# A fused three-layer kernel: eight gate tiles moved ahead of a barrier or into an attention's last heads, and one norm's steps drawn later

## The chip, the cores and the metric

The kernel runs on one core of one Trainium2 chip. The metric is the time of one execution on the device, in microseconds (us). The engines are PE (TensorE, matmuls), PEld (its weight loads), DVE (VectorE), ACT (ScalarE), POOL (GpSimd) and SP (which issues most DMA). TensorE's clock is either 1.2 or 2.4 GHz; the profile gives the granted clock of a stretch as a share of the full one.

## The reference, cut to what matters

A first block (one hybrid layer on 512 tokens and 16 meta tokens in front, width 1024), then two latent layers that work on 512 tokens and a context of 256:

```python
h = h + 0.5 * swiglu(rmsnorm(h, norm_ffn1), w_ffn1_in, w_ffn1_out)
u = rmsnorm(h, norm_mix)
fq, fk, fv, ff, rq, rk, rv, rg, ga, gb = split(u @ w_in)
y_a = forgetting_attention(rms(fq), rms(fk), fv, log_sigmoid(ff + b))   # "fox": 16 heads of 64
y_b = silu(rg) * head_groupnorm(retention(rotary(rq), rotary(rk), rv))  # 4 heads, values 256 wide
mixed = sigmoid(ga + b_gate[:D]) * (y_a @ w_o_fox) + sigmoid(gb + b_gate[D:]) * (y_b @ w_o_ret)
h = h + mixed @ w_out
h = h + 0.5 * swiglu(rmsnorm(h, norm_ffn2), w_ffn2_in, w_ffn2_out)
# then, for l in 0, 1: modulate (a LayerNorm without gain, times 1 + scale, plus shift), the projection
# w_in_2, three kinds of mixing, w_o_2, LayerNorm, and a swiglu between two more norms
```

## The kernel before, in words

Activations lie transposed: 128 features on the partitions, 8 blocks of them, tokens along the free axis. A product of such an activation by a weight matrix is made tile by tile: a weight tile has 128 output features and all 8 blocks of input (128x1024 numbers). Every fp32 product is three fp32r matmuls, high by high, high by low and low by high (`mm3`, L1134 to L1137), so a tile of 8 blocks over 512 tokens is 24 matmuls of 512 columns, and one over 256 tokens (a "chunk") 24 of 256.

A weight tile goes through three engines before PE may use it. SP loads it into a ring of four buffers (`Wf`), ACT rounds it to its high half (L1744, `Wbaseh`, `Wtoph`, `Wlatenth` by the region it goes to), DVE subtracts that from the whole and leaves the low half (L2366, `Wbasel`, ...). Both emit the split of a tile in the program order of their own queue, one tile ahead of PE's use of it (`get`), so a split stands in line with whatever else ACT and DVE do at that place.

Each engine has a class that writes its queue by the same method names (`retention`, `mix`, `hooks`), and semaphores tie them together. The order around three places matters here.

**Retention.** The rotated queries and keys (`RQ`, `RK`) and the values (`VR`) are ready behind a barrier (`bar("rot")`, which waits for DVE's and ACT's last writes). Then PE makes 16 scores (L1488, L1490), each for one head and one block of 128 queries, and one step later the output of that unit, once DVE has multiplied the scores by the decay table `DT`. The 8 tiles of the gate `silu(rg)` (weights `w_rg`, 512 tokens) depend on none of this and stand in front of every second output.

**Fox attention and mix.** 64 units, one for each head (16) and block of 128 queries (4). A unit goes round a loop: scores on PE (L1586 to L1589), row maximum on DVE (L2870), exp on ACT (L2118), scaling by the sum on DVE (L2886, `Pb`), transposition on PE (L1601, L1602), copies on ACT (L2132, `PT`; L2133, `MT`). The transposition of unit u stands behind the scores of unit u+1 or so, and after the fourth unit of a head comes the product with the values (L1629). Steps of the projections and norms of later heads are hung between the scores and what follows by lists of hooks (`FOX_PLAN`, run by `hooks`); behind unit 51 hardly any of them are left. Behind the last head comes the mix: for each of the two branches 8 times a gate tile (`w_ga` or `w_gb`, 512 tokens, input `X1`) and an output tile (`w_of` with the attention's output `YA`, or `w_or`), then ACT's sigmoid and DVE's product.

**The norm before the second latent sequence.** Here a planner (`woven`) lays the steps of three LayerNorms (`mean`, `mu`, `sq`, `var`; means L1339, totals L1361, on ones in `CF`) between weight tiles: each chain has a tile after which it may start and a delay in us by which its steps fall due. `FILL` says how many dummy matmuls (L1123, output unused) PE makes in front of a named step, so that it stays busy while it waits. The norm `a0` has chunk 0 for the context and chunks 1 and 2 for the latent tokens; behind chunk 2's last step stand 16 tiles of 256 columns with the normed tokens `X2`, of which the later ones need `X2`'s second half.

Of the kernel before, what the change touches and what calls it, by code (L numbers as in the profile page):

```python
# [502 lines left out]
class Ffn:  # L503
# [12 lines left out]
    def ends(self, c, ci=None):  # L516


        if ci == 2 and self.tag[0] == "g":
# [13 lines left out]
FOX_OWN = (0, 14)  # L533
FOX_CH = {"q": LAT, "k": TWO}
FOX_FIRST = [[("refine", "q", 0), ("root", "k", 0)], [("scale", "q", 0), ("refine", "k", 0)],
             [("root", "k", 1), ("scale", "k", 0)], [("refine", "k", 1), ("scale", "k", 1)]]
# [85 lines left out]
def qk_before(l, s, c):  # L622
# [3 lines left out]

FILL = {("fa", "f1", 0, 0): 7, ("yb", 6): 4, ("mean", "a0", 1): 11, ("mu", "a0", 2): 13, ("hm", 0, 0, 0): 2,
# [173 lines left out]
def second_sequence(p):  # L801

    f, n3, a = p.ffns["f2"], p.norms["n3"], p.norms["a0"]
    items = [(("open", "mixed", [(p.mm, ("branch", 1, 7, 0))]), 0, None)]
    items += [(("wo", m, c), 2.8, None) for m, c in lagged(range(8), 2, 4)]
    ends = [last_of(items, "wo", c, None) for c in (0, 1)]
    items[8:8] = [(("ahead", 2), 0, None)]
    items += [(("close", "mixed"), 0, None), (("open", "top", [(p.mm, ("mixout", 7, 1))]), 0, None)]
    items.append((("vectors", 1), 0, None))
    tiles = ffn_items(f, 4, lambda c: c, mod_steps(1))  # L810
    items += tiles[:8] + [(("ahead", AHEAD), 0, None)] + tiles[8:]
    done = last_of(items, "fb", 1, f)
    ends += [last_of(items, "fo", c, f) for c in (0, 1)]
    items += [(("close", "top"), 0, None), (("open", "latent", [(p.mm, ("fo", "f2", 2, 7, 1))]), 0, None)]
    items += projection_items(0, lambda c: 2 + c)
    chains = [(chain([n3], c), ends[c], 1.9) for c in (0, 1)] + [(chain([a], 0), done, 0.0)]
    chains += [(chain([a], c + 1), ends[2 + c], 0.8) for c in (0, 1)]
    return woven(items, chains)
# [75 lines left out]
class FoxUnits:  # L894
    def __init__(self, p):
        self.p, self.id, self.l, self.units, self.joined, self.lag, self.slots = p, "fox", None, [], True, 2, 4
        late = fox_steps(False)
        for h in range(16):
            sel, v = p.SEL[:, h, :].bitcast(BF16), h // 2 * 128
            for i in range(4):  # L900
# [12 lines left out]
                d.head_done = i == 3  # L913
                d.hooks = [("fox", *x[1:]) for x in late if x[0] == 4 * h + i]
                self.units.append(d)
# [170 lines left out]
class TensorE(Engine):  # L1086
# [369 lines left out]
    def retention(self):  # L1456
        p, e = self.p, self.e
        for s in range(4, 12):
# [6 lines left out]
            if s <= 8:  # L1465
                self.ret_turn(s - 1)
        self.bar("rot")
        e.wait_ge(*p.dve.of(("bar", "rot")))
        e.wait_ge(*p.act.of(("bar", "rot")))
        for u in range(17):  # L1470
            if u < 16:
                self.ret_scores(u)
                if u % 2 == 0:
                    self.lin("w_rg", (u // 2,), 8, p.X1, 0, [(16, 512)], ("rg", u // 2),
                             lambda c: (p.act, ("rg", u // 2)))
            if u >= 1:
                self.ret_out(u - 1)
        self.features(p.YT, range(4), range(8), ("yb",), lambda f: (p.dve, ("yb", f)),
                      lambda f: [(p.dve, ("gn", f // 2, 3))])
        self.bar("yb")  # L1480

    def ret_scores(self, u):
# [44 lines left out]
    def fox_step(self, m, f, *a):  # L1527
        if f == "project":
            self.project(a[0], m, *a[1:])
        elif f == "root":  # L1530
            self.root(a[0], m, a[1])
        elif f == "stack" and 2 * m + a[0] not in FOX_OWN:
            self.p.stacks[2 * m + a[0]] = self.used + AHEAD + NW + 1
# [87 lines left out]
    def head_values(self, A, u):  # L1621
# [8 lines left out]
        t.then_inc(*p.mm.did(("c", A.id, h)))  # L1630

    def mix(self):
        p, e = self.p, self.e
        for br, (wg, wo, Y) in enumerate((("w_ga", "w_of", p.YAs), ("w_gb", "w_or", p.YBs))):
            for m in range(8):
                self.lin(wg, (m,), 8, p.X1, 0, LAT, ("gate", br, m), lambda c: (p.act, ("gate", br, m)))
                self.lin(wo, (m,), 8, Y, 16, LAT, ("branch", br, m), lambda c: (p.dve, ("branch", br, m)),
                         (lambda c0, n, k: [(p.dve, ("ysplit", br, k))]) if m == 0 else None)
            if br == 0:
                self.bar("m1")  # L1640
# [89 lines left out]
class ScalarE(Engine):  # L1730
# [313 lines left out]
    def fox_step(self, m, f, *a):  # L2044
        if f == "project":
            self.project(a[0], m, *a[1:])
        elif f == "root":
            self.root(a[0], m, a[1])
        elif f == "stack":
            self.stack(2 * m + a[0])  # L2050

    def project(self, which, m, i, k0, k1):
# [108 lines left out]
    def mix(self):  # L2161
        p, e = self.p, self.e
        for br, (wg, wo, Y, S, G) in enumerate((("w_ga", "w_of", p.YAs, p.YA, p.GT),
# [3 lines left out]
            for m in range(8):  # L2167
                self.lin(wg, (m,))
                self.lin(wo, (m,))
# [185 lines left out]
class VectorE(Engine):  # L2355
# [440 lines left out]
    def fox_step(self, m, f, *a):  # L2796
# [4 lines left out]
        elif f == "scale":  # L2801
            self.head_scale(a[0], m, a[1])
        elif f == "stack" and 2 * m + a[0] in FOX_OWN:
            self.stack(2 * m + a[0])

    def stack(self, h):
# [5 lines left out]
        e.tensor_tensor(p.KL[o:o + 64, s, :], p.K[r0:r0 + 64, m % 2, :], p.KS[r0:r0 + 64, s, :].bitcast(F32),  # L2812
                        ALU.subtract).then_inc(*p.dve.did(("sk_low", h)))

    def project(self, which, m, i, k0, k1):
# [129 lines left out]
    def mix(self):  # L2945
        p, e = self.p, self.e
        for br, (wg, wo, Y, S, G) in enumerate((("w_ga", "w_of", p.YAs, p.YA, p.GT),
# [3 lines left out]
            for m in range(8):  # L2951
                self.lin(wg, (m,))
                self.lin(wo, (m,))
# [663 lines left out]
```

## Time and profile before

| | us |
|---|---|
| median of 3 runs | 3371.64 (3370.69 to 3379.82) |
| the profiled execution, its own time | 3374.06 |
| its span, first to last instruction | 3372.0 |
| DVE busy | 1695.1 (50%) |
| ACT busy | 1333.7 (40%) |
| POOL busy | 475.1 (14%) |
| mean granted clock of TensorE | 0.995 |

The span is what the trace covers; 2.1 us of the execution lie outside it. The times of the trace count from the span's start. PE is busy nearly all of the time, so the stretches in which it has no real work are few: idle gaps, dummy matmuls, and stretches at half clock. A row of the timeline shows in brackets how long its engine was idle before it and which instruction ended that.

### The profile page before, as it was taken

The page shows a single profiled execution, that of the slowest core. Times are in us where ns is not written, and L with a number is a line of the kernel's source. Part 1 is how long each engine was busy: PE and PEld are TensorE (multiplying, and loading weights), DVE is VectorE, ACT ScalarE, POOL GpSimd, SP SyncE. Part 2 cuts the span into 40 slices and gives each one's busy share as a digit, 9 for nine tenths or more (in the row PEclk, how much of TensorE's full clock was granted, in tenths as well). Part 3 has the DMA queues.
Part 4 walks back from the last instruction along what each step waited for, and adds up shares of the span by engine and source line. Part 5 has one row for each costly group of instructions (what it writes and reads, how often), then busy time and mean ns, then how long its engine had stood idle before and what let it go on. Part 6 is the DMA issues. An engine that isn't in the chain of part 4 may idle for free. (4 is left out here: it accounts for less than half of the span.)

```text
span 3372.0 us, 60102 instructions
## 1 busy us (share of the span) xinstructions
PE 3268.7 (97%) x24738; PEld 3046.1 (90%) x24754; DVE 1695.1 (50%) x2839; ACT 1333.7 (40%) x2350; POOL 475.1 (14%) x471
## 2 busy tenths in 40 slices
PE   8999999999899999999999999999999999999998
PEld 7999988887678999998889889999998889999997
DVE  4666643546634456666445773222227646743234
ACT  4222322346633332225347664212125547552224
POOL 1010110036400010010013201001010114110100
PEclk9999999999999999999999999999999999999999
DMA  4444422122122244443201431111214212423222
GB/s 162 159 171 172 138 82 76 54 74 66 36 88 94 100 136 177 169 170 99 67 30 38 128 101 57 63 57 58 69 56 133 85 55 48 152 70 91 91 93 91
DMA packets 94973, 325.23 MB, mean 96 GB/s; under 512 B 10800, under 2 KB 15152, under 8 KB 94576
## 3 DMA queue, kind: packets, MB, share of 16 engines
q1 hardware_dynamic: 90992, 307.19, 28.1%
q0 software_dynamic: 3280, 13.68, 1.2%
q8 instruction: 199, 3.26, 0.4%
q14 instruction: 70, 0.57, 0.1%
q10 hardware_dynamic: 432, 0.52, 0.0%
HBM read 309.96 MB, written 2.10 MB: 93 GB/s over the span
## 5 line engine op out<-in xcount | busy, mean ns | idle before, releaser
L2366 DVE TENSOR_TENSOR r_Wbasel<-r_Wf,r_Wbaseh 128x1024 fp32r<-128x1024 f32 (+1 forms) x298 | 378.0, 1269 | 549.8 <-ACT r_Wbaseh L1744 549.3
L1744 ACT ACTIVATE r_Wbaseh<-r_Wf 128x1024 fp32r<-128x1024 f32 (+1 forms) x298 | 308.4, 1039 | 447.1 <-PE PS L1137 351.4
L1135 PE MATMUL PS<-r_X1h,r_Wbaseh 128*128 128x264 f32 (+2 forms) x1216 | 392.0, 322 | 13.1 <-POOL r_X1l L3192 3.4
L1135 PE MATMUL PS<-r_X2h,r_Wbaseh 128*128 128x256 f32 (+1 forms) x1224 | 373.8, 305 | 5.7 <-POOL r_X2l L3192 3.1
L1136 PE MATMUL PS<-r_X1l,r_Wbaseh 128*128 128x264 f32 (+2 forms) x1216 | 378.6, 311 | 0.0
L1137 PE MATMUL PS<-r_X1h,r_Wbasel 128*128 128x264 f32 (+2 forms) x1216 | 378.0, 311 | 0.0
L1137 PE MATMUL PS<-r_X2h,r_Wbasel 128*128 128x256 f32 (+1 forms) x1224 | 366.7, 300 | 0.0
L1136 PE MATMUL PS<-r_X2l,r_Wbaseh 128*128 128x256 f32 (+1 forms) x1224 | 364.3, 298 | 0.0
L2366 DVE TENSOR_TENSOR r_Wtopl<-r_Wf,r_Wtoph 128x1024 fp32r<-128x1024 f32 (+1 forms) x165 | 200.1, 1214 | 275.9 <-ACT r_Wtoph L1744 275.7
L1135 PEld LDWEIGHTS PS<-r_X1h,r_Wbaseh 128*128 128x128 f32 x1216 | 230.1, 189 | 37.4 <-issue 8.7
L1135 PE MATMUL PS<-r_X2h,r_Wtoph 128*128 128x256 f32 x872 | 248.1, 285 | 2.1 <-POOL r_X2l L3192 2.1
L1135 PEld LDWEIGHTS PS<-r_X2h,r_Wbaseh 128*128 128x128 f32 x1224 | 230.8, 189 | 19.6 <-POOL r_X2l L3192 4.3
L1137 PE MATMUL PS<-r_X2h,r_Wtopl 128*128 128x256 f32 x872 | 247.4, 284 | 0.0
L1136 PE MATMUL PS<-r_X2l,r_Wtoph 128*128 128x256 f32 x872 | 247.4, 284 | 0.0
L1136 PEld LDWEIGHTS PS<-r_X1l,r_Wbaseh 128*128 128x128 f32 x1216 | 230.4, 189 | 14.5 <-issue 2.4
L1137 PEld LDWEIGHTS PS<-r_X1h,r_Wbasel 128*128 128x128 f32 x1216 | 230.7, 190 | 13.0
L1136 PEld LDWEIGHTS PS<-r_X2l,r_Wbaseh 128*128 128x128 f32 x1224 | 232.7, 190 | 10.4 <-issue 2.6
L1137 PEld LDWEIGHTS PS<-r_X2h,r_Wbasel 128*128 128x128 f32 x1224 | 230.0, 188 | 7.9
L1744 ACT ACTIVATE r_Wtoph<-r_Wf 128x1024 fp32r<-128x1024 f32 (+1 forms) x165 | 168.7, 1027 | 169.0 <-PE PS L1137 83.9
L1951 ACT ACTIVATE r_TM<-PS 128x256 f32<-128x256 f32 (+1 forms) x198 | 76.0, 385 | 339.0 <-PE PS L1137 334.0
L1135 PE MATMUL PS<-r_X1h,r_Wtoph 128*128 128x264 f32 (+1 forms) x672 | 190.4, 283 | 4.7 <-DVE r_Wtopl L2366 4.6
L2615 DVE TENSOR_TENSOR r_TM<-r_TM,PS 128x256 f32<-128x256 f32 (+1 forms) x198 | 83.3, 421 | 216.7 <-PE PS L1137 203.7
(428 smaller groups left out, 9078.5 us busy)
## 6 DMA issues: line engine op xcount, KB each, us to landing
r_Wf<-in_wmod SPq DMA_DIRECT2D x96, 512.0 KB, 3.6
r_Wf<-in_f_in SPq DMA_DIRECT2D x88, 512.0 KB, 4.4
r_Wf<-in_g_in SPq DMA_DIRECT2D x88, 512.0 KB, 3.5
r_Wf<-in_g_out SPq DMA_DIRECT2D x56, 448.0 KB, 3.3
r_Wf<-in_w_o SPq DMA_DIRECT2D x40, 512.0 KB, 4.3
r_Wf<-in_f_out SPq DMA_DIRECT2D x32, 448.0 KB, 4.2
r_Wf<-in_f_out SPq DMA_DIRECT2D x16, 512.0 KB, 4.4
r_Wf<-in_w_v SPq DMA_DIRECT2D x16, 512.0 KB, 3.5
```

The source lines that it names most:

```text
L1135: self.e.matmul(o, wh, xh, start=first, stop=False)
L1136: self.e.matmul(o, wh, xl, start=False, stop=False)
L1137: return self.e.matmul(o, wl, xh, start=False, stop=last)
L1744: e.activation(p.w(i, cols)[0], p.Wf[:, i % NW, 0:cols], ACT.Copy).then_inc(*p.hi.did(i))
L1951: e.activation(f.tm(c), p.psb(p.bank(("fa", f.tag, j, c)), f.chunks[c][1]), ACT.Silu).then_inc(*p.act.did(("silu", f.tag, j, c)))
L2366: e.tensor_tensor(l, p.Wf[:, i % NW, 0:cols], h.bitcast(F32), ALU.subtract).then_inc(*p.lo.did(i))
L2615: e.tensor_tensor(x, x, p.psb(p.bank(("fb", f.tag, j, c)), f.chunks[c][1]), ALU.mult).then_inc(*p.dve.did(("gated", f.tag, j, c)))
```

## The change

Three places are written in another order; nothing of the computation changes, and the number of real matmuls is the same.

**Retention.** `ret_gate(m)` makes one gate tile. Tile 0 now stands ahead of the barrier's waits, and tiles 1 to 7 stand behind the scores of units 1, 3, ... 13 in place of 2, 4, ... 14. ACT's and DVE's queues are not touched.

**Fox and mix.** The gate tiles 0 and 1 of branch 0 are made inside the attention's last three heads, each in four quarters of 6 matmuls, behind the scores of units 52 to 55 (tile 0) and 57, 60, 62 and 63 (tile 1). In the mix, gate tile m+2 runs beside output tile m, and output tiles 5, 6 and 7 follow each other. A tile that is got inside a unit brings a weight split with it, the one of the tile after it, which ACT and DVE now make in units 52 and 57.

**The norm a0.** The delays of its chunks 1 and 2 go from 0.8 us to 5.5 and 9.0 us, the 11 dummy matmuls in front of ("mean", "a0", 1) are gone, and those in front of ("mu", "a0", 2) go from 13 to 11.

```diff
@@ -532,6 +532,8 @@
+FOX_GATE = [(u, m, "gate", k, k + 2) for u, m, k in
+            [(52, 0, 0), (53, 0, 2), (54, 0, 4), (55, 0, 6), (57, 1, 0), (60, 1, 2), (62, 1, 4), (63, 1, 6)]]
@@ -624,7 +626,7 @@
-FILL = {("fa", "f1", 0, 0): 7, ("yb", 6): 4, ("mean", "a0", 1): 11, ("mu", "a0", 2): 13, ("hm", 0, 0, 0): 2,
+FILL = {("fa", "f1", 0, 0): 7, ("yb", 6): 4, ("mu", "a0", 2): 11, ("hm", 0, 0, 0): 2,
@@ -814,7 +816,7 @@
     chains = [(chain([n3], c), ends[c], 1.9) for c in (0, 1)] + [(chain([a], 0), done, 0.0)]
-    chains += [(chain([a], c + 1), ends[2 + c], 0.8) for c in (0, 1)]
+    chains += [(chain([a], c + 1), ends[2 + c], (5.5, 9.0)[c]) for c in (0, 1)]
     return woven(items, chains)
@@ -911,7 +913,7 @@
-                d.hooks = [("fox", *x[1:]) for x in late if x[0] == 4 * h + i]
+                d.hooks = [("fox", *x[1:]) for x in late + FOX_GATE if x[0] == 4 * h + i]
@@ -1465,19 +1467,22 @@
         self.bar("rot")
+        self.ret_gate(0)
         e.wait_ge(*p.dve.of(("bar", "rot")))
         e.wait_ge(*p.act.of(("bar", "rot")))
         for u in range(17):
             if u < 16:
                 self.ret_scores(u)
-                if u % 2 == 0:
-                    self.lin("w_rg", (u // 2,), 8, p.X1, 0, [(16, 512)], ("rg", u // 2),
-                             lambda c: (p.act, ("rg", u // 2)))
+                if u % 2 and u < 15:
+                    self.ret_gate(u // 2 + 1)
             if u >= 1:
                 self.ret_out(u - 1)
...
+    def ret_gate(self, m):
+        self.lin("w_rg", (m,), 8, self.p.X1, 0, [(16, 512)], ("rg", m), lambda c: (self.p.act, ("rg", m)))
@@ -1629,11 +1636,30 @@
+    def mix_gate(self, m, k0, k1):
+        p, e = self.p, self.e
+        c0, n = LAT[0]
+        if k0 == 0:
+            self.half = self.get("w_ga", (m,), 1024)
+            e.wait_ge(*p.lo.of(self.half))
+            self.half_bank = self.take(("gate", 0, m, 0), (p.act, ("gate", 0, m)))
+        u = self.half
+        wh, wl = p.w(u, 1024)
+        for k in range(k0, k1):
+            t = self.mm3(p.psb(self.half_bank, n), wh[:, k * 128:k * 128 + 128], wl[:, k * 128:k * 128 + 128],
+                         p.X1[0][:, k, c0:c0 + n], p.X1[1][:, k, c0:c0 + n], k == 0, k == 7)
+        if k1 == 8:
+            t.then_inc(*p.mm.did(("gate", 0, m, 0), ("w", u)))
+            self.finished(u)
     def mix(self):
...
             for m in range(8):
-                self.lin(wg, (m,), 8, p.X1, 0, LAT, ("gate", br, m), lambda c: (p.act, ("gate", br, m)))
+                g = m if br else m + 2
+                if g < 8:
+                    self.lin(wg, (g,), 8, p.X1, 0, LAT, ("gate", br, g), lambda c: (p.act, ("gate", br, g)))
                 self.lin(wo, (m,), 8, Y, 16, LAT, ("branch", br, m), lambda c: (p.dve, ("branch", br, m)),
@@ -2046,8 +2072,17 @@
+    def mix_gate(self, m, k0, k1):
+        if k0 == 0:
+            self.half = self.get("w_ga", (m,), 1024)
+        if k1 == 8:
+            self.finished(self.half)
...
```

What PE has at the barrier in front of the retention's scores, before. `RQ`, `RK` are the rotated queries and keys, `X1h`, `X1l` the halves of the normed input; L1136 to L1137 with 256 columns are the last value tile.

```order
L1136 MATMUL PS<-r_Wbasel,r_X1h 128x256
L1137 MATMUL PS<-r_Wbaseh,r_X1l 128x256
L1488 MATMUL PS<-r_RQ,r_RK 128x128
L1490 MATMUL PS<-r_RQ,r_RK 16x128
L1135 MATMUL PS<-r_X1h,r_Wbaseh 128x512
```

The same place after (L1138 and L1139 are L1136 and L1137 of before; 24 matmuls of 512 columns begin at the third row).

```order
L1138 MATMUL PS<-r_Wbasel,r_X1h 128x256
L1139 MATMUL PS<-r_Wbaseh,r_X1l 128x256
L1137 MATMUL PS<-r_X1h,r_Wbaseh 128x512
L1138 MATMUL PS<-r_X1l,r_Wbaseh 128x512
L1139 MATMUL PS<-r_X1h,r_Wbasel 128x512
```

The whole gate tile has moved in front of the first scores, which stood directly behind the barrier.

ACT in unit 57 before: the two stack copies of a later head (L2093, L2094), then the copies of unit 56's transposed weights, then the exp of unit 57.

```order
L2093 ACTIVATE r_QS<-r_Q 64x512
L2094 ACTIVATE r_KS<-r_K 64x528
L2132 ACTIVATE r_PT<-PS 128x512
L2133 ACTIVATE r_MT<-PS 16x128
L2118 ACTIVATE r_Pb,r_SM<-PS,r_SM 128x272
```

And after, where L2128, L2129, L2167, L2168 and L2153 are these five and L1770 is the split's high half.

```order
L2128 ACTIVATE r_QS<-r_Q 64x512
L2129 ACTIVATE r_KS<-r_K 64x528
L1770 ACTIVATE r_Wbaseh<-r_Wf 128x1024
L2167 ACTIVATE r_PT<-PS 128x512
L2168 ACTIVATE r_MT<-PS 16x128
L2153 ACTIVATE r_Pb,r_SM<-PS,r_SM 128x272
```

A split of 128x1024 has come in front of the two copies and the exp. Another stands so in unit 52, and DVE has its half of each in front of that unit's maximum.

PE before, at the mean of a0's chunk 1: the end of an ffn tile, the mean's first four blocks, the dummies, its last four, and the next tile (`H2` is the ffn's inner activation, `H` the residual).

```order
L1136 MATMUL PS<-r_H2l,r_Wtoph 128x256
L1137 MATMUL PS<-r_H2h,r_Wtopl 128x256
L1339 MATMUL PS<-r_H,r_CF 32x256 x4
L1123 MATMUL PS<-r_CF 128x256 x11
L1339 MATMUL PS<-r_H,r_CF 32x256 x4
L1135 MATMUL PS<-r_H2h,r_Wtoph 128x256
```

After (L1341 is L1339 of before), with two tiles more ahead of it.

```order
L1138 MATMUL PS<-r_H2l,r_Wtoph 128x256
L1139 MATMUL PS<-r_H2h,r_Wtopl 128x256
L1341 MATMUL PS<-r_H,r_CF 32x256 x8
L1137 MATMUL PS<-r_H2h,r_Wbaseh 128x256
L1138 MATMUL PS<-r_H2l,r_Wbaseh 128x256
```

The dummies are gone and the mean stands behind two further tiles. In tiles (f is one of the ffn's last, # one of the 16 with `X2`), the rest of the stretch read before: mean 1 with dummies, f, mu 1, f, f, sq 1, f, var 1, #1, mean 2, #2, dummies, mu 2, #3, #4, sq 2, #5, var 2, #6 to #16; it reads now: f, f, mean 1, f, mu 1, f, #1, sq 1, #2, var 1, #3, mean 2, #4, dummies, mu 2, #5, #6, sq 2, #7, var 2, #8 to #16. ACT's split of #10 stood behind the two halves of chunk 2's `X2`, with two more splits in front; it has now been made before them.

## Rows read from the trace of the kernel before

**Rows 1.** The page's busy times: us, share of the span, instructions.
```profile
PE 3268.7 (97%) x24738; PEld 3046.1 (90%) x24754; DVE 1695.1 (50%) x2839; ACT 1333.7 (40%) x2350; POOL 475.1 (14%) x471
```
**Rows 2.** PE's timeline at the retention's barrier: start, us, instruction, [idle before, releaser].
```profile
538.68 0.49 PE L1488 MATMUL PS<-r_RQ,r_RK 128*128 128x128 f32 x2 [2.04 <-DVE r_VR L2676]
...
541.38 0.63 PE L1135 MATMUL PS<-r_X1h,r_Wbaseh 128*128 128x512 f32 x1
541.81 0.63 PE L1136 MATMUL PS<-r_X1l,r_Wbaseh 128*128 128x512 f32 x1
```
**Rows 3.** DVE's timeline: the gate tile's low half, and the last value copy.
```profile
524.36 1.20 DVE L2366 TENSOR_TENSOR r_Wbasel<-r_Wf,r_Wbaseh 128x1024 fp32r<-128x1024 f32 x1
...
537.56 1.07 DVE L2676 COPY r_VR<-PS 16x256 f32<-16x256 f32 x3
```
**Rows 4.** PE by windows: us, PE busy, granted clock, DMA share, GB/s.
```profile
540.00:544.00 4.00, 4.00 (x12) 0.57 0.85 301
...
898.00:903.00 5.00, 4.59 (x27) 0.66 0.00 0
903.00:926.00 23.00, 16.42 (x127) 1.00 0.06 13
926.00:933.00 7.00, 7.00 (x28) 0.51 0.01 2
```
**Rows 5.** PE's timeline: start of the second gate tile of the mix, and of the tile behind it.
```profile
942.06 0.39 PE L1135 MATMUL PS<-r_X1h,r_Wbaseh 128*128 128x512 f32 x1
...
947.64 0.39 PE L1135 MATMUL PS<-r_YAh,r_Wbaseh 128*128 128x512 f32 x1
```
**Rows 6.** PE's waits from 893 to 928 us: in total, times, longest.
```profile
PE PS L1601 <- DVE r_Pb L2886: 4.9, 4, 1.5
PE PS L1629 <- ACT r_MT L2133: 2.3, 3, 1.0
PE PS L1601 <- ACT r_MT L2133: 1.4, 3, 0.8
PE PS L1586 <- ACT r_MT L2133: 0.7, 1, 0.7
```
**Rows 7.** PE's timeline in the last heads and the first mix tile.
```profile
898.41 0.41 PE L1601 MATMUL PS<-r_CF,r_Pb 128*128 128x128 f32 x2 [1.22 <-DVE r_Pb L2886]
...
910.36 0.87 PE L1629 MATMUL PS<-r_PT,r_VF 128*64 128x256 f32 x7 [1.02 <-ACT r_MT L2133]
...
925.81 2.19 PE L1629 MATMUL PS<-r_PT,r_VF 128*64 128x256 f32 x14 [0.93 <-ACT r_MT L2133]
...
928.97 0.79 PE L1135 MATMUL PS<-r_X1h,r_Wbaseh 128*128 128x512 f32 x1
...
936.45 0.40 PE L1135 MATMUL PS<-r_YAh,r_Wbaseh 128*128 128x512 f32 x1
```
**Rows 8.** ACT's timeline: unit 57's second stack copy and exp, and a split.
```profile
908.82 0.62 ACT L2094 ACTIVATE r_KS<-r_K 64x528 fp32r<-64x528 f32 x1
...
910.24 0.49 ACT L2118 ACTIVATE r_Pb<-PS,r_SM 128x272 f32<-128x272 f32 x1
...
1568.29 1.04 ACT L1744 ACTIVATE r_Wbaseh<-r_Wf 128x1024 fp32r<-128x1024 f32 x1
```
**Rows 9.** PE's timeline around the norm a0's chunks 1 and 2.
```profile
1540.10 5.02 PE L1123 MATMUL PS<-r_CF 128*128 128x256 f32 x22
1545.57 0.64 PE L1339 MATMUL PS<-r_H,r_CF 128*32 128x256 f32 x8 [0.46 <-DVE r_H L2627]
...
1565.16 5.78 PE L1123 MATMUL PS<-r_CF 128*128 128x256 f32 x26
1571.82 0.70 PE L1361 MATMUL PS<-r_PA,r_CF 128*128 128x256 f32 x2 [0.88 <-ACT r_PA L1858]
...
1596.81 0.39 PE L1135 MATMUL PS<-r_X2h,r_Wlatenth 128*128 128x256 f32 x1 [2.44 <-DVE r_Wlatentl L2366]
```
**Rows 10.** DVE's timeline: two low halves in that stretch.
```profile
1542.55 2.54 DVE L2366 TENSOR_TENSOR r_Wbasel<-r_Wf,r_Wbaseh 128x1024 fp32r<-128x1024 f32 x1 [2.12 <-ACT r_Wbaseh L1744]
...
1594.20 2.55 DVE L2366 TENSOR_TENSOR r_Wlatentl<-r_Wf,r_Wlatenth 128x1024 fp32r<-128x1024 f32 x1 [2.79 <-ACT r_Wlatenth L1744]
```

More of the change, by code:

```diff
@@ L1531, in fox_step @@
             self.root(a[0], m, a[1])
+        elif f == "gate":
+            self.mix_gate(m, *a)
         elif f == "stack" and 2 * m + a[0] not in FOX_OWN:
@@ L2048, in fox_step @@
             self.root(a[0], m, a[1])
+        elif f == "gate":
+            self.mix_gate(m, *a)
         elif f == "stack":
             self.stack(2 * m + a[0])
+    def mix_gate(self, m, k0, k1):
[3 more added lines that the diff above has]
+            self.finished(self.half)
     def project(self, which, m, i, k0, k1):
@@ L2167, in mix @@
             for m in range(8):
-                self.lin(wg, (m,))
+                g = m if br else m + 2
+                if g < 8:
+                    self.lin(wg, (g,))
                 self.lin(wo, (m,))
@@ L2802, in fox_step @@
             self.head_scale(a[0], m, a[1])
+        elif f == "gate":
+            self.mix_gate(m, *a)
         elif f == "stack" and 2 * m + a[0] in FOX_OWN:
@@ L2813, in stack, with mix_gate @@
                         ALU.subtract).then_inc(*p.dve.did(("sk_low", h)))
+    def mix_gate(self, m, k0, k1):
+        if k0 == 0:
+            self.half = self.get("w_ga", (m,), 1024)
+        if k1 == 8:
+            self.finished(self.half)
     def project(self, which, m, i, k0, k1):
@@ L2951, in mix @@
             for m in range(8):
-                self.lin(wg, (m,))
+                g = m if br else m + 2
+                if g < 8:
+                    self.lin(wg, (g,))
                 self.lin(wo, (m,))
```

## The prediction

> **What bounds the kernel now.** I read the page's busy times first. PE is busy 97% of the span, DVE 50%, ACT 40% and POOL 14% [rows 1]. So only what PE does or waits for at the three places can move the end, and all that DVE, ACT and SP do there costs nothing unless PE comes to wait for it. The number of real matmuls doesn't change. A gain can come from three sources: idle time of PE, dummy matmuls, and stretches at the clock's lower level. Then I read the timeline and the windows at each place. At the retention's barrier PE is idle for 2.04 us and afterwards runs four us at a mean clock of 0.57 [rows 2, 4]. In the last heads of the attention it waits 4.9 + 2.3 + 1.4 + 0.7 = 9.3 us in 11 waits, for the scaled probabilities and for the copies of their transposes [rows 6]. Around the norm a0 it makes dummies for 5.02 and 5.78 us and is idle for 0.46, 0.88 and 2.44 us [rows 9].
>
> The sum is made against the profiled execution, 3374.06 us, whose span is 3372.0 and which lies 2.4 us above the median of the runs shown, 3371.64.
>
> **Part A, the retention's gate tiles.** Before, PE ends the last value tile at 536.64 (538.68 less 2.04) and waits for DVE's last value copy, 537.56 + 1.07 [rows 2, 3]. After, gate tile 0 stands there. Its low half is ready at 524.36 + 1.20 = 525.56 [rows 3], so it starts at once. A gate tile of 24 matmuls takes 947.64 - 942.06 = 5.58 us at full clock [rows 5], so it runs to 542.2, past the barrier's release at 538.7. The idle 2.04 goes. What goes with it is the fall of the clock: the matmuls behind the gap follow each other in 541.81 - 541.38 = 0.43 us where 5.58 / 24 = 0.233 is the full rate, and the window of 4 us loses 4 x (1 - 0.57) = 1.7 [rows 2, 4]. Once PE is busy through the place I see nothing to lower the clock, and count 1.6 of it. The scores now come 3.5 us later than before, but the load of the decay table is issued by POOL behind the same barrier as before and is not later, and 5.6 us of gate work stand behind each second score as they did, so DVE's product and the outputs keep their cover. At the end one gate tile less stands behind unit 14; the head norm's chain there belongs to the last outputs, which PE follows with the features' work, and I count nothing. A = 3.6; from below 2.0 (the gap alone), from above 3.7.
>
> **Part B, the gates of the mix inside the last heads.** Two tiles, 2 x 5.58 = 11.2 us, leave the mix [rows 5]. The question is how much they lengthen the tail. Eight quarters of 6 matmuls, 6 x 0.233 = 1.40 us each, meet 9.3 us of idle time, and it is the loop through DVE and ACT that sets the pace there, not PE: it is busy 16.42 of 23 us [rows 4]. What lengthens the loop itself are the two splits and the quarters that stand between a unit's scores and the transposition that is already due.
>
> Unit 52: the high half takes 1.04 on ACT [rows 8], the low half 1.20 on DVE [rows 3], and DVE's stands ahead of the unit's maximum. The scaled probabilities of the unit before, on which the transposition at 898.41 waits, are made by DVE behind it [rows 7]; I walk this as 1.3 later. This lateness then stays: the quarters of 53, 54 and 55 lie in gaps (0.8 to 2.0 late at the transpositions, 1.3 again at the last one in front of unit 57).
>
> Unit 57: ACT has the high half behind the stack copy that ends at 909.44, and ahead of the exp at 910.24 [rows 8]. With the 1.3 it runs 910.9 to 911.95, DVE's low half to 913.2, and only then come the maximum and the exp of the unit. The product with the values of head 13, before at 910.36 [rows 7], comes at 912.9, 2.5 late, and the exp at 913.7, 3.5 late. So the split adds 1.2 there.
>
> Units 60, 62 and 63: the quarters stand behind the scores, and the idle time in front of the transpositions [rows 6] hides part of them; walking scores, maximum, exp, scaling, transposition and copies from unit to unit gives the product of head 14 3.8 late, and of head 15, before at 925.81 [rows 7], 930.7, 4.9 late: 1.3 + 1.2 + 2.7 of quarters, less 0.3 absorbed.
>
> Before, the clock is low from 926 to 933 at 0.51 [rows 4], and the first mix tile takes 936.45 - 928.97 = 7.48 us [rows 7] instead of 5.58. I take it that the fall comes again, since the gaps in front of it stay, and only moves. B = 11.2 - 4.9 = 6.3. The bounds: if the tail gets no longer and the clock stays full, 11.2 + 7 x (1 - 0.51) = 3.4 less what the lesser share of idle takes back, at most 14.4; if all quarters and both splits stand in series, 8 x 1.40 + 2 x (1.04 + 1.20) = 15.7, so 11.2 - 15.7 = -4.5. In the mix itself output tiles 5, 6 and 7 come back to back, with one weight split per 5.58 us on ACT (1.04) and DVE (1.20), which is ample.
>
> Here a rule of the Trainium skill can be weighed. The windows show 0.66, then 1.00 for 23 us in which PE is busy for 16.42, then 0.51 [rows 4], so the clock fell twice in a stretch full of short gaps, and once it held. The Trainium skill, "TensorE: Matmul & The Clock Gate", section "HAM oscillation — how this bites in real kernels", has it that a loop that waits again and again throttles the engine again and again. By that rule the fall at the tail recurs as long as the gaps do, and the sum stands as it is; by the opposite reading, that eight quarters fill enough of the gaps, B would be 9.5, the first rival below.
>
> **Part C, the norm a0.** What is not work there, before: from 1540.10 to the mean at 1545.57 is 5.47; from 1565.16 to the total at 1571.82 is 6.66; and 2.44 at the tile #10; together 14.57 [rows 9]. After: the mean of chunk 1 stands two ffn tiles later; a tile of 21 matmuls of 256 columns, at half of 0.233 each, is 2.5 us, so PE is there at about 1544.6 (its first half stood 0.57 in front of 1540.10 before). The residual that it reads is made by DVE behind a slow low half, 1542.55 + 2.54 = 1545.1 [rows 10], and comes at 1545.57 less what the mean's first half covers, so 0.43 of idle are left where 5.47 were. The steps sq 1 and var 1 have one tile each between them, with 0.1 of wait. The mean of chunk 2 comes at 1561.45 and tile #4 runs to 1565.3; the total mu 2 needs ACT's sum, which stands behind chunk 1's `X2` high halves and a split as before and comes at 1571.4, so 6.1 of dummies and waiting remain. sq 2 waits 0.4. At #10 the split that came late, the low half 1594.20 to 1596.75 [rows 10], is made before `X2`'s last halves, and the 2.44 go. Left: 0.43 + 0.2 + 6.1 + 0.4 = 7.1. C = 14.57 - 7.1 = 7.5. What is late next is chunk 2's second half of `X2` at tile #14: ready at 1595.9 by the walk, wanted at 1599.2. The bounds: if the chain falls as late as its new delay says (9.0 - 0.8 = 8.2, against 3.3 of margin) 4.9 come back, 2.5 left; at most the whole 14.6.
>
> **The sum.** 3.6 + 6.3 + 7.5 = 17.4 us less than the profiled execution, 3356.7; less 2.4 for how that stands to the median: 3354.2. With all three at their best 3.7 + 14.4 + 14.6 = 32.7 (3338.9); at their worst 2.0 - 4.5 + 2.5 = 0.0.
>
> **Rivals.**
> 1. The clock stays full at the end of the tail, because the quarters fill the gaps. For it: between 903 and 926 it stayed at 1.00 with PE busy 71% [rows 4], and the quarters raise that share. Against it: three of the gaps of about 1 us ahead of 925.81 are behind the last quarter or not covered by it. The low clock gives 3.4 back, less 0.2: total 20.6, 3351.0.
> 2. The tail takes all that the mix gives. Each quarter stands in front of a transposition that is due, and every split lengthens the loop, so that 11.2 go back in series. For it: the loop through DVE and ACT bounds the tail, and a new link in it is not hidden by PE's idle time. Against it: 9.3 us of idle [rows 6]. B = 0, total 11.1, 3360.5.
> 3. The norm's chain of chunk 2 comes late at #14. C = 2.5, total 12.4, 3359.2. For it: the delay grows by 8.2 us and 16 tiles stand behind the chain; against it: 3.3 of margin in the walk.
> 4. Slower than before: the clock stays low through the whole tail. PE's busy time of 903 to 926 then runs double, and so do the eight quarters: 16.4 + 11.2 = 27.6 us more. B = 6.3 - 27.6 = -21.3, total 3.6 - 21.3 + 7.5 = -10.2, 3381.8. It decides from 17.4 us of additional time at the low clock. For it: a late split in unit 52 adds a gap right where the clock is at 0.66 already [rows 4]. Against it: quarters are dense matmuls where there was nothing.
> 5. The change hardly does what it says: the gaps reappear one step further on at all three places (retention's outputs, mix, #14), total near 3, 3369.
>
> **How the numbers follow.** The forecast has 0.42, the rivals 0.20, 0.16, 0.11, 0.04 and 0.07. The range leaves out rival 4, rival 5 and a little of either side of the others: 3346 to 3366. No change means within 0.3%, some 10 us, which is about what a measurement of this kernel can tell; faster is below 3361.5. The forecast and rival 1 are faster throughout (0.61 of 0.62), rivals 2 and 3 lie 1 to 2.3 us inside the line, so two thirds of them (0.18). Same: the other third (0.09) and rival 5 (0.07), with 0.01 of the forecast. Slower: 0.04.
>
> **What would show it.** A: no idle time in front of the scores at the barrier, and a clock of 1.00 in the 4 us behind it. B: quarters of 1.4 us behind the scores of the units named; the product of head 15 some 5 us later relative to the first scores of unit 52; a first mix tile (now gate 2) that still takes over 7 us, and with 5.6 rival 1 is right. C: no dummies in front of mean 1, the weights of #10 ready, and no wait at #14 (if one of some 5 us stands there, rival 3). The prediction is wrong if the tail from unit 52 to the first mix tile grows by over 11 us, or if a window of the tail shows a low clock that was not there.

## The result

The changed kernel takes 3354.27 us (median of 4 runs, 3352.92 to 3356.47) against 3373.51 (4 runs, 3370.69 to 3379.82). The ratio is 0.9943, with a 95% interval of 0.9928 to 0.9958: 19.2 us less, where 17.4 had been forecast. The profiled execution took 3353.84 us with a span of 3352.0, so its span is 20.0 us shorter than that of before.

The page's busy times after, which answer to [rows 1]:

```profile
PE 3258.5 (97%) x24712; PEld 3038.8 (91%) x24728; DVE 1694.5 (51%) x2839; ACT 1330.2 (40%) x2350; POOL 474.8 (14%) x471
```

PE does 10.2 us less: 5.9 are the 11 dummies of the first mean and the two fewer in front of the total (5.02, and 5.78 - 4.91), the rest is mostly less time at the lower clock. The other 9.8 of the 20 us were idle time.

At the barrier (PE's timeline after; [rows 2] before) the gate tile starts at 536.77 and the scores follow it with no idle time:

```profile
536.77 0.39 PE L1137 MATMUL PS<-r_X1h,r_Wbaseh 128*128 128x512 f32 x1
...
542.34 0.38 PE L1493 MATMUL PS<-r_RQ,r_RK 128*128 128x128 f32 x2
```

PE by windows after (us, PE busy, granted clock, DMA share, GB/s). The first four answer to [rows 4]; the last three lie elsewhere, and what they mean is told below.

```profile
540.00:544.00 4.00, 4.00 (x22) 1.00 0.85 304
...
898.00:903.00 5.00, 5.00 (x36) 1.00 0.06 24
903.00:926.00 23.00, 20.07 (x136) 1.00 0.12 36
926.00:933.00 7.00, 5.59 (x36) 1.00 0.01 2
...
1160.00:1168.00 8.00, 7.05 (x58) 1.00 0.00 0
...
1704.00:1708.00 4.00, 4.00 (x23) 0.57 0.00 0
1728.00:1732.00 4.00, 3.92 (x16) 0.57 0.00 0
```

The tail after ([rows 7] before): the products with the values of heads 13 and 15, then the first gate tile of the mix, which now takes 935.66 - 929.96 = 5.70 us and not 7.48.

```profile
909.32 1.30 PE L1636 MATMUL PS<-r_PT,r_VF 128*64 128x256 f32 x14 [0.81 <-ACT r_MT L2168]
...
928.15 1.30 PE L1636 MATMUL PS<-r_PT,r_VF 128*64 128x256 f32 x14 [0.93 <-ACT r_MT L2168]
...
929.96 0.50 PE L1137 MATMUL PS<-r_X1h,r_Wbaseh 128*128 128x512 f32 x1
...
935.66 0.40 PE L1137 MATMUL PS<-r_YAh,r_Wbaseh 128*128 128x512 f32 x1
```

The norm a0 after ([rows 9] before): the mean's two halves, the dummies and the total of chunk 2, and the total of its squares; no tile behind them waits.

```profile
1531.34 0.64 PE L1341 MATMUL PS<-r_H,r_CF 128*32 128x256 f32 x8
1532.45 0.64 PE L1341 MATMUL PS<-r_H,r_CF 128*32 128x256 f32 x8 [0.47 <-DVE r_H L2664]
...
1552.84 4.91 PE L1125 MATMUL PS<-r_CF 128*128 128x256 f32 x22
1557.98 0.70 PE L1363 MATMUL PS<-r_PA,r_CF 128*128 128x256 f32 x2 [0.23 <-ACT r_PA L1884]
...
1568.38 0.60 PE L1363 MATMUL PS<-r_PA,r_CF 128*128 128x256 f32 x2
```

Between these two profiles the stretches gave 3.8 (the retention), 8.2 (the tail and the mix, to its second branch) and 9.2 us (around the norm). Elsewhere, where both programs have the same order, 1.2 us went (the window at 1162 to 1170 of before is at 0.79, the one of after at 1.00) and 2.5 came back (the windows at 1704 and 1728 of after at 0.57; before has no low clock between 1169 and 2004). So a part of any such pair is the clock's chance, and the experiments had to say which part.

### The profile page after: what moved, and what is told of

The parts are those of the page before. It is cut to its first block and busy times, and to the rows that moved or that the text cites. A ratio compares the mean times of both kernels' runs of the same rounds, so it can differ in the third digit from the quotient of the medians.

```text
span 3352.0 us, 60050 instructions
## 1 busy us (share of the span) xinstructions
PE 3258.5 (97%) x24712; PEld 3038.8 (91%) x24728; DVE 1694.5 (51%) x2839; ACT 1330.2 (40%) x2350; POOL 474.8 (14%) x471
## 5 line engine op out<-in xcount | busy, mean ns | idle before, releaser
L1770 ACT ACTIVATE r_Wbaseh<-r_Wf 128x1024 fp32r<-128x1024 f32 (+1 forms) x298 | 308.1, 1037 | 441.5 <-PE PS L1139 340.5
L1137 PE MATMUL PS<-r_X1h,r_Wbaseh 128*128 128x264 f32 (+2 forms) x1216 | 390.4, 321 | 12.5 <-POOL r_X1l L3240 3.4
L1137 PE MATMUL PS<-r_X2h,r_Wbaseh 128*128 128x256 f32 (+1 forms) x1224 | 373.8, 305 | 5.6 <-POOL r_X2l L3240 3.1
L1138 PE MATMUL PS<-r_X1l,r_Wbaseh 128*128 128x264 f32 (+2 forms) x1216 | 376.3, 309 | 0.0
L1139 PE MATMUL PS<-r_X1h,r_Wbasel 128*128 128x264 f32 (+2 forms) x1216 | 376.1, 309 | 0.0
L1139 PE MATMUL PS<-r_X2h,r_Wbasel 128*128 128x256 f32 (+1 forms) x1224 | 366.5, 299 | 0.0
L1138 PE MATMUL PS<-r_X2l,r_Wbaseh 128*128 128x256 f32 (+1 forms) x1224 | 364.0, 297 | 0.0
L1137 PEld LDWEIGHTS PS<-r_X1h,r_Wbaseh 128*128 128x128 f32 x1216 | 228.5, 188 | 35.1 <-issue 8.1
L1137 PE MATMUL PS<-r_X2h,r_Wtoph 128*128 128x256 f32 x872 | 248.1, 285 | 2.1 <-POOL r_X2l L3240 2.1
L1137 PEld LDWEIGHTS PS<-r_X2h,r_Wbaseh 128*128 128x128 f32 x1224 | 230.6, 188 | 20.0 <-POOL r_X2l L3240 4.3
L1139 PE MATMUL PS<-r_X2h,r_Wtopl 128*128 128x256 f32 x872 | 247.5, 284 | 0.0
L1138 PE MATMUL PS<-r_X2l,r_Wtoph 128*128 128x256 f32 x872 | 247.4, 284 | 0.0
L1138 PEld LDWEIGHTS PS<-r_X2l,r_Wbaseh 128*128 128x128 f32 x1224 | 232.7, 190 | 10.5 <-issue 2.6
L1138 PEld LDWEIGHTS PS<-r_X1l,r_Wbaseh 128*128 128x128 f32 x1216 | 229.0, 188 | 14.0 <-issue 2.4
L1139 PEld LDWEIGHTS PS<-r_X1h,r_Wbasel 128*128 128x128 f32 x1216 | 229.1, 188 | 12.6
L1139 PEld LDWEIGHTS PS<-r_X2h,r_Wbasel 128*128 128x128 f32 x1224 | 229.8, 188 | 7.9
L1770 ACT ACTIVATE r_Wtoph<-r_Wf 128x1024 fp32r<-128x1024 f32 (+1 forms) x165 | 168.5, 1026 | 166.1 <-PE PS L1139 84.0
L1137 PE MATMUL PS<-r_X1h,r_Wtoph 128*128 128x264 f32 (+1 forms) x672 | 191.0, 284 | 4.9 <-DVE r_Wtopl L2403 4.8
```

The lines of the kernel that those rows point to most:

```text
L1137: self.e.matmul(o, wh, xh, start=first, stop=False)
L1138: self.e.matmul(o, wh, xl, start=False, stop=False)
L1139: return self.e.matmul(o, wl, xh, start=False, stop=last)
L1770: e.activation(p.w(i, cols)[0], p.Wf[:, i % NW, 0:cols], ACT.Copy).then_inc(*p.hi.did(i))
```

## The experiments

In the expectations "changed kernel" is the one above and "before" the one it came from. Distances in us are of single profiles; times are medians and ratios are to before, from 5 to 11 executions of each variant and 9 to 23 of before (`before_again` and `after2` are one each), with the 95% interval in brackets. "The tail" is the attention's last heads, behind head 11.

**Each part alone, and the kernel before once more.** In `a_only` the diff's hunks of `retention` alone are kept, in `c_only` those of `FILL` and of `chains`, in `b_only` all others. For `b_only` this is the change less

```diff
-        self.ret_gate(0)
-FILL = {..., ("mu", "a0", 2): 11, ...}
+FILL = {..., ("mean", "a0", 1): 11, ("mu", "a0", 2): 13, ...}
-    chains += [(chain([a], c + 1), ends[2 + c], (5.5, 9.0)[c]) for c in (0, 1)]
+    chains += [(chain([a], c + 1), ends[2 + c], 0.8) for c in (0, 1)]
```

> Part A alone (gate tiles of the retention one place sooner), the rest as before. Theory: the idle 2.04 us in front of the first scores and the low clock behind it both go, and PE reaches the attention's last heads 3.7 us sooner; the time falls by 3.7 us (ratio 0.9989). Rival: the low clock behind the gap has nothing to do with the gap and comes somewhere near it anyway; then 2.0 us. In the profile: windows 540 to 548 at 1.00 by the theory.

> Part B alone (gate tiles 0 and 1 of the mix in quarters in the last heads). Theory: the product of head 15 comes 6 us late against the first scores of unit 52, 11.2 us leave the mix, and the clock stays at 1.00 at the end of the tail because the quarters fill its gaps: -8.2 us (ratio 0.9976), the first mix tile 5.7 us long. Rival: the quarters are not what kept the clock up, the level there is chance; then the first mix tile can again be 7 us or more and the gain is 5 us.

> Part C alone (the norm a0's chains later, fewer dummies). Theory: PE ends the 16 tiles behind the norm 9.2 us sooner and nothing of this is given back: -9.2 us (ratio 0.9973). Rival: the 2.6 us that the whole change lost again some 110 us behind the norm, in windows at a granted clock of 0.72, belong to C; then -6.6 us, and the same two windows are low again.

> The kernel before, once more, for its profile. If the low clock at the retention's barrier (0.57), at the tail's end (0.51) and behind the LayerNorm's wait near 1165 (0.66) stand there again, each belongs to its gap; if the gaps are the same and a low window is gone or another has come, the level after such a gap is partly chance. Theory: the first two are there again, the third need not be. Rival: all three are as before.

`a_only` 3370.63, ratio 0.9988 (0.9979 to 0.9997): 4.0 us less. `b_only` 3368.66, 0.9984 (0.9975 to 0.9993): 5.4 less. `c_only` 3365.07, 0.9970 (0.9959 to 0.9982): 10.1 less. Together 19.5 against 19.2 for the whole; each of the three is known to 3 or 4 us only, so this agreement shows no more than that no large part is missing.

Windows of `before_again` (columns as above):

```profile
540.00:544.00 4.00, 4.00 (x15) 0.80 0.76 270
896.00:900.00 4.00, 2.79 (x14) 0.58 0.00 0
900.00:904.00 4.00, 4.00 (x21) 0.50 0.00 0
904.00:908.00 4.00, 4.00 (x20) 0.64 0.01 2
926.00:933.00 7.00, 6.84 (x40) 1.00 0.01 2
1592.00:1596.00 4.00, 3.93 (x21) 0.62 0.57 151
```

The same program had its low clock at other places: longer in 896 to 908, none at the tail's end (where it was expected again), one at 1592 that the first profile did not have. The gap of 2.04 us at the barrier was there in all six profiles without part A, and a low clock behind it in three (`before`, `before_again`, `b_splits`). From the end of the last value tile to the first tile behind the retention it was 101.9 us with the low clock (those three), 100.4 without (`b_only`, `c_only`; 100.7 in `b_dummy`), and 98.1 in all eight profiles with part A. So the gap is worth 2.3 us in each execution and the clock 1.5 in about half of them: 3.0 on average. The rival of `a_only`, that the low clock comes anyway, falls: no profile with part A has one there.

In `b_only` the clock was low at the tail's end, against the theory:

```profile
896.00:904.00 8.00, 6.84 (x49) 1.00 0.18 66
912.00:920.00 8.00, 6.69 (x40) 0.79 0.36 102
932.00:940.00 8.00, 7.08 (x30) 0.57 0.01 2
```

`c_only` took 64.7 us from the first half of the mean to the latent norm's sums (L1692), as did the changed kernel; with the two ffn tiles that now stand ahead of the mean (4.95) that is 69.6, against 78.8 in two profiles without part C and 80.3 in four. The four have a low clock behind the wait of 2.4 us at the tile #10, as in the last row of `before_again`; with part C there is neither the wait nor the low clock. So C is 9.2 in each execution and 10.2 on average. The 2.5 us given back behind 1700 in the changed kernel were not there in `c_only`, so the rival falls.

**Part B taken apart.** `b_splits` gets the two weight tiles in units 52 and 57 and makes their 48 matmuls at the start of the mix; `b_dummy` leaves the mix as before and puts dummies where the quarters stand.

```diff
# b_splits, in mix_gate, for k0 == 0:
+            self.kept.append(self.get("w_ga", (m,), 1024))
# b_dummy, in mix_gate, and g = m in mix:
+        for _ in range(3):
+            t = e.matmul(p.PS[:, self.half_bank, 256:512], p.ONES, p.CF[:, 0:2, :], start=True, stop=True)
```

> As part B alone, but only the weight splits stay in units 52 and 57 (with the two tiles' loads and slots); the 48 matmuls of the two gate tiles run at the start of the mix, so PE's work is that of before. Theory: the splits are what lengthens the loop at units 52 and 57, by 1.3 + 1.2 = 2.5 us at the product of head 15, and nothing leaves the mix: +2.5 us (ratio 1.0007). Rival: PE's quarters in front of the transpositions cost all of the 6 us and the splits lie in gaps of ACT and DVE; then 0.

> The kernel before with dummy matmuls of the same length (3 of 256 columns in fp32, some 1.37 us) where the eight quarters stand, the mix unchanged, no splits moved. Theory: quarters alone lengthen the tail by 6.0 - 2.5 = 3.5 us and do not keep the clock up: +3.5 us (ratio 1.0010), and low windows between 893 and 936 are still seen. Rival: the quarters keep the clock up; then no window below 0.95 there, and about 0 (3.5 against some 4 us of low clock that go).

`b_splits` 3374.43, 1.0000 (0.9991 to 1.0009); `b_dummy` 3377.19, 1.0012 (1.0003 to 1.0020).

The trace of `b_splits` shows that it does only half of what was intended. Its first split stands in unit 52, as in the changed kernel. But both gate tiles are held until the mix, and the split that was to stand in unit 57 comes only there, once a matmul of PE has ended (ACT's timeline; head 15's product is at 929.92):

```profile
897.18 1.05 ACT L1775 ACTIVATE r_Wbaseh<-r_Wf 128x1024 fp32r<-128x1024 f32 x1
...
937.67 1.06 ACT L1775 ACTIVATE r_Wbaseh<-r_Wf 128x1024 fp32r<-128x1024 f32 x1 [0.49 <-PE PS L1139]
```

So `b_splits` measures the first split alone. The times are too coarse for such sizes, so the profiles are compared by two distances: from head 11's product with the values to head 15's, and from there to the first output tile of the second branch.

| profile | head 11 to 15 | to branch 2 | windows under 0.95, of 893 to 940 |
|---|---|---|---|
| before | 35.69 | 100.04 | around 896 to 903, 924 to 934 |
| before_again | 36.96 | 96.92 | 896 to 908 |
| a_only | 36.06 | 96.91 | 904 to 908 |
| c_only | 37.01 | 96.88 | 892 to 908 |
| b_splits | 38.79 | 96.88 | 900 to 912 |
| b_dummy | 38.61 | 96.91 | none |
| b_only | 43.16 | 88.57 | 912 to 920, 932 to 940 |
| after | 41.77 | 85.76 | none |
| after2 | 41.79 | 88.69 | 928 to 936 |
| no_fill | 41.80 | 88.76 | 928 to 936 |
| plus1 | 41.30 | 90.09 | 924 to 940 |
| plus2 | 41.31 | 88.81 | 928 to 936 |
| plus2_58 | 40.81 | 88.82 | 924 to 936 |
| plus2_53 | 40.16 | 85.72 | none |

The mix gives 96.9 - 85.76 = 11.1 us, as forecast. The tail grows from 36.4 (mean of the first four) to 41.9 (mean of the six of `b_only` to `plus2`), by 5.4. The dummies alone make it 2.2 longer than that mean, and the one split of `b_splits` 2.4. The clock is in both numbers: `b_splits` had the long low clock, and is 1.8 longer than the two at 37.0 that had it too; `b_dummy` had none, and is 2.6 to 2.9 longer than the two with a short one (36.1 and 35.7). So the quarters and the first split both count, and neither costs all; the second split is in neither run, and the rest is left for it. For `b_dummy` the sign that its rival named came true (no low window in the tail), but not its time: it takes 4.0 us more (1.0 to 6.7), as the theory had it.

The low clock changes place: without the quarters it came within 20 us behind head 11's product in all four profiles, where the loop waits on DVE and ACT anyway (35.7 and 36.1 us with a short one, 37.0 twice with a long one); with the quarters that part is at 1.00 in all eight, and the low clock comes in the last gaps in six of eight, where the 24 dense matmuls of the mix's first tile follow and 2.8 to 4.3 us are lost. By sums of the two distances part B gave 134.1 - 130.3 = 3.8 us on average (four profiles and six), within the 5.4 (2.4 to 8.4) of `b_only`'s time. The 8.2 between the first two profiles was a poor draw for before and a lucky one for after.

**The changed kernel once more, and without its dummies.**

> The changed kernel once more, for its profile. Theory: which gaps are followed by a low clock is partly chance; in the first profile none was in the last heads, and part B with three others gave a low window at the tail's end three times in three. So a low window between 893 and 936 is likely, and the stretch from the product of head 11 to the second branch's first output tile takes 130 to 132 us instead of 127.5. Rival: the changed kernel as a whole keeps that stretch at full clock; then 127.5 again.

> The changed kernel without the 11 dummy matmuls in front of the total mu of the norm a0's chunk 2: PE is idle for some 5.1 us there. Theory: the total comes at the same time, and the gap, longer than the others, is followed by a low clock in each run, which costs 1.5 to 1.7 us of the tiles behind it (ratio to before 0.9948). Rival: the dummies do nothing for the clock; then the time is that of the changed kernel (0.9943) and no low window stands behind 1558.

```diff
-FILL = {..., ("mu", "a0", 2): 11, ...}
+FILL = {..., ...}
```

`after2` took 3356.84 and had its low clock at the tail's end, window 926 to 933 (and 1.00 from 893 to 926); 130.5 us for the stretch, as the theory had it. `no_fill` 3360.18, 0.9954 (0.9941 to 0.9968), which holds the theory's 0.9948 and the rival's 0.9943 alike, so its profile has to decide. In its timeline and windows:

```profile
1562.32 1.19 PE L1363 MATMUL PS<-r_PA,r_CF 128*128 128x256 f32 x2 [5.08 <-ACT r_PA L1884]
```
```profile
1560.00:1568.00 8.00, 5.68 (x27) 0.57 0.32 95
```

The total comes as late with 5.08 us of idle time as with dummies, and the eight us behind it are at 0.57. From the mean to the latent sums it took 66.94 us instead of 64.66 and 64.69: in this profile the dummies are worth 2.3 us, and the theory holds with a size of half as much again. That the low clock comes in each execution is not shown by one.

**More tiles in front of the total, and the gates at other units.** `plus1` and `plus2` put one and two projection tiles more in front of the total; `plus2_58` and `plus2_53` are `plus2` with other units.

```diff
# plus1: 3.0 and 4 dummies; plus2: 5.8 and none
+    chains[-1][0][0] = (*chains[-1][0][0][:2], 5.8)
# plus2_58; plus2_53 has also 53, 54, 55, 56 for 52, 53, 54, 55
-            [(52, 0, 0), (53, 0, 2), (54, 0, 4), (55, 0, 6), (57, 1, 0), (60, 1, 2), (62, 1, 4), (63, 1, 6)]]
+            [(52, 0, 0), (53, 0, 2), (54, 0, 4), (55, 0, 6), (58, 1, 0), (60, 1, 2), (62, 1, 4), (63, 1, 6)]]
```

> The changed kernel with one more projection tile in front of the total mu of the norm a0's chunk 2, and 4 dummies there in place of 11. Theory: the total comes at the same time, the tile (2.9 us) takes the place of dummies, and the normed chunk 2 is still ready (1582.0 against 1583.1 in the profile of the changed kernel): 2.9 us less than the changed kernel (ratio to before 0.9934). Rival: the chain comes later by what ACT and DVE do for the additional tile, and PE waits for it at the 14th tile; then no gain.

> The changed kernel with two more projection tiles in front of that total and no dummies. Theory: 5.1 us of dummies and waiting go, 0.6 come at the total, and the 14th tile waits 1 to 2 us for the normed chunk: 3.5 us less than the changed kernel (ratio to before 0.9932). Rival: the chain is late by a whole tile; then 0 to 1 us less than the changed kernel.

> The version with two more tiles in front of the total (plus2), and the second gate tile begun at unit 58 instead of 57. In 57 POOL multiplies a stack of keys for 1.30 us at the moment when DVE makes the split's low half, and that took 2.23 us where 1.20 is the usual; in 58 POOL has nothing. Theory: the low half takes 1.2 us and the tail from the product of head 11 to that of head 15 is 1 us shorter (40.3 against 41.3). Rival: the length of the low half is not due to POOL, or the split is as much in the way in 58; then 41.3 or more.

> As plus2_58, and the first gate tile in units 53 to 56 instead of 52 to 55. In 52 a norm's last steps on POOL meet the split's low half, and one of the two took 1.83 us. Theory: both are short in 53, but the gap of unit 52 (1.5 us) is then not filled; from the product of head 11 to that of head 15 some 39.5 to 41 us. Rival: unit 52's gap was the best cover, and the tail gets longer, 42.

`plus1` 3354.44, 0.9944 (0.9931 to 0.9956); `plus2` 3351.85, 0.9934 (0.9922 to 0.9947). From the mean's first half to the latent sums they took 63.26 and 61.88 against 64.7, so they gain 1.4 and 2.8 and not 2.9 and 3.5. Part of what they won at the total is waited for at a tile whose low half is late and at the next step, the squares, which no theory had; the wait at the 14th tile that the theory of `plus2` had is not there (PE's timeline of `plus2`):

```profile
1564.07 0.39 PE L1138 MATMUL PS<-r_X2h,r_Wbaseh 128*128 128x256 f32 x1 [0.88 <-DVE r_Wbasel L2404]
1570.78 0.64 PE L1342 MATMUL PS<-r_SQ,r_CF 128*32 128x256 f32 x8 [0.69 <-ACT r_SQ L1897]
1571.82 0.64 PE L1342 MATMUL PS<-r_SQ,r_CF 128*32 128x256 f32 x8 [0.40 <-ACT r_SQ L1897]
```

`plus2_58` 3350.92, 0.9932 (0.9919 to 0.9944); `plus2_53` 3350.93, 0.9929 (0.9917 to 0.9941). The tail went from 41.31 to 40.81 and 40.16: shorter, by 0.5 where 1.0 was expected for the first, and by 0.65 for the second. DVE's low halves say why. In `plus2` they take 1.23 and 2.25 us, in `plus2_53` 1.23 and 1.23. In `plus2_58` the second takes 1.23 as expected, but the first, which nothing in the program moved, takes 0.6 longer than in `plus2`:

```profile
892.84 1.83 DVE L2404 TENSOR_TENSOR r_Wbasel<-r_Wf,r_Wbaseh 128x1024 fp32r<-128x1024 f32 x1 [0.36 <-ACT r_Wbaseh L1771]
```

So the 1.0 was gained and about half of it lost again at unit 52. All the intervals of `plus1` to `plus2_53` overlap with that of the changed kernel. By the profiles the two last gain 2.8 at the norm and 1.0 and 1.6 in the tail against the changed kernel; their times, 3350.92 and 3350.93, can't be told apart.

## Why the prediction was right, and where it was not

The time was within 0.1 us of the forecast 3354.2, and that closeness is luck. The forecast started from a median of 3371.64 for the kernel before, which came out at 3373.51, so the gain is 19.2 (14.2 to 24.3) and not 17.4; one execution of the kernel before differs from the next by up to 9 us; and the errors of the parts below nearly cancel: A and B were too high, C too low. The mechanisms of A and C are shown, the one of B in part.

**Part A**: the gap went as worked out, 2.3 us for 2.04. The 1.6 of the clock were counted in full; the low clock follows the gap in three of six profiles and costs 1.5, so the term should have been some 0.75. The measured 4.0 (1.0 to 7.1) can't tell 3.6 from 3.0.

**Part B**: forecast 6.3, measured 3.8 by the profiles and 5.4 by the time. Two steps were off. The first is "DVE's low half to 913.2" in unit 57, and the like in 52: both were priced at 1.20. Here are DVE's low halves and POOL's work in the changed kernel:

```profile
893.51 1.82 DVE L2403 TENSOR_TENSOR r_Wbasel<-r_Wf,r_Wbaseh 128x1024 fp32r<-128x1024 f32 x1 [0.37 <-ACT r_Wbaseh L1770]
908.58 2.23 DVE L2403 TENSOR_TENSOR r_Wbasel<-r_Wf,r_Wbaseh 128x1024 fp32r<-128x1024 f32 x1 [2.66 <-ACT r_Wbaseh L1770]
```
```profile
893.50 0.76 POOL L3300 TENSOR_TENSOR r_RS<-r_RS,r_RS 128x264 f32<-128x264 f32 x1
...
908.43 1.30 POOL L3313 TENSOR_TENSOR r_KL<-r_K,r_KS 64x528 fp32r<-64x528 f32 x1
```

In both POOL had begun a product of two operands 0.01 and 0.15 us sooner, and DVE's instruction ends 1.07 and 1.08 us behind POOL's end (895.33 to 894.26, 910.81 to 909.73): it was done after it, not beside it. That makes them 0.6 and 1.0 us longer. Against the first profile of before the products of heads 13, 14 and 15 came 2.7, 5.0 and 6.1 us late, where the walk had 2.5, 3.8 and 4.9: the miss opens behind the split of unit 57. In `plus2_58`, where the second split meets nothing on POOL, it is 1.23 us:

```profile
909.15 1.23 DVE L2404 TENSOR_TENSOR r_Wbasel<-r_Wf,r_Wbaseh 128x1024 fp32r<-128x1024 f32 x1 [2.99 <-ACT r_Wbaseh L1771]
```

The sign of it stood in [rows 10]: two low halves of 2.54 and 2.55 us that I read as "slow" without asking why. The Trainium skill, "GPSIMD Engine Reference", section "8. Key points", says that GpSimd shares its SBUF interfaces with VectorE and that VectorE's instructions with two SBUF inputs contend; the trace agrees, 1.82 and 2.23 us against 1.23.

The second is "I take it that the fall comes again". It does, in six of eight profiles with the quarters. But the 0.51 in [rows 4], against which the gain was reckoned, is itself rare without the quarters: one profile in five. The forecast took it on both sides of the difference, so it fell out of the sum, where the profiles have it in one of five against six of eight, at some 3 us each time. Numbers this small, and `b_dummy` with dummy quarters and none, don't show that the quarters cause it. Rival 1 looked right from the first pair of profiles (5.70 us for the first mix tile, and the prediction's own test said so) and is refuted as a rule by `b_only` and `after2`; that the clock stays full at the tail's end remains the case in two of eight. That a loop which waits again and again throttles TensorE again stood in the prediction from the Trainium skill, "TensorE: Matmul & The Clock Gate", section "HAM oscillation — how this bites in real kernels", whose own case has longer waits; here six of eight profiles agree with it, and two don't. Rival 2, a tail that gives everything back, would have grown by 11.2; it grew by 5.4. Rival 4 needed 17.4 us at the low clock; the most lost in one tail is some 5 (10.2 us at half clock).

**Part C**: forecast 7.5, measured 9.2, and 10.2 with the clock. The step mis-sized was what is left: 5.68 us (0.47 of idle and 0.07 beside it at the mean, 5.14 at the total) in place of 7.1, which makes 8.9; 0.3 are not accounted for. The total came 9.12 us behind chunk 2's mean, where the walk had 9.95, and the waits of 0.4 and 0.2 at the squares and the variances were not there. The prediction had the right number and did not use it: its walk wants tile #14 at 1599.2, and before it starts at 1608.41, 9.2 later. Rival 3 fell: POOL's half of the normed chunk is ready at 1582.04 and tile #14 starts at about 1586.0, 4.0 us of margin where I had 3.3. The clock behind the wait at #10, low in four of six profiles without part C, was not in the sum; it adds 1.0.

So A was about 0.6 too high, B 0.9 to 2.5 too high, C 2.7 too low. Rival 5, a gain near 3, is out by the interval.

## What to carry to other kernels

Where an engine is idle for a microsecond or two here, count the gap at its length and the lower clock behind it as a chance (some 1.5 us each time; the odds went with the place, from three in six to every profile), and take a second profile of the unchanged kernel before you reckon with the clock in the first. An instruction moved to another place has the duration of its new neighbours: look at what POOL does at that moment before you price DVE's. Dummies that fill a known wait were worth 2.3 us for 5.1; real tiles in their place were worth 1.4 each. And look in the trace whether an experiment moved what it was to move, as `b_splits` did not, before you subtract its number.

## What the runs showed of the hardware

Profiles in which a stretch has the same order and the same gaps to 0.1 us differ in whether TensorE's clock falls to its lower level, 1.2 GHz, behind the gap: behind 2.04 us of idle in three of six, behind 2.4 at the tile #10 in four of six, behind 2.43 at a later projection tile (1725.79 in before) in nine of fourteen, behind 5.08 in the one profile of it. The length of the gap alone doesn't give the odds: two other gaps of 2.1 us are followed by it in all fourteen profiles. In before these are

```profile
2004.04 0.67 PE L1361 MATMUL PS<-r_PA,r_CF 128*128 128x256 f32 x2 [2.14 <-ACT r_PA L1858]
...
2966.14 0.39 PE L1135 MATMUL PS<-r_X2h,r_Wtoph 128*128 128x256 f32 x1 [2.07 <-POOL r_X2l L3192]
```

What differs at these places no run here takes apart.

A low half on DVE and a product of two operands on POOL that overlap are done one after the other. Of the 5418 low halves of 128x1024 in the fourteen profiles 366 took over 1.4 us, where 1.2 is the usual; all 366 end 1.08 or 1.09 us behind the end of such a product on POOL, however long the two overlap (in before, 1541.65 + 2.36 = 1544.01 and 1545.09, 1593.29 + 2.38 = 1595.67 and 1596.75). When DVE is the first, it is POOL's that is longer. Which of the two is held up can turn on less than the profile resolves: in `plus1`, and so in `plus2`, DVE's first low half took 1.23 and POOL's product 1.83, where the changed kernel and `plus2_58` have 1.82 or 1.83 and 0.76, and in all of them the two starts are within 0.01 us of each other. The tail is 0.5 us shorter where POOL is the one held up (41.3 against 41.8).

```profile
893.57 1.23 DVE L2404 TENSOR_TENSOR r_Wbasel<-r_Wf,r_Wbaseh 128x1024 fp32r<-128x1024 f32 x1 [0.36 <-ACT r_Wbaseh L1771]
```
```profile
893.56 1.83 POOL L3301 TENSOR_TENSOR r_RS<-r_RS,r_RS 128x264 f32<-128x264 f32 x1
```
